# A two-layer attention and mixture-of-experts kernel: down products in other pieces, norm rows spread by TensorE

## The reference

```python
for layer in range(2):
    h = attention[layer](x)
    x = layernorm(ALPHA * x + h, ln_g[layer, 0], ln_b[layer, 0])
    f = moe(x, w_gate[layer], w_up[layer], w_down[layer])
    x = layernorm(ALPHA * x + f, ln_g[layer, 1], ln_b[layer, 1])

def moe(t):                       # combine: two gates a token, chosen by a router
    for e in range(32):           # w_gate, w_up: 1024 x 256, w_down: 256 x 1024
        h = silu(t @ w_gate[e]) * (t @ w_up[e])
        y = y + combine[:, e:e + 1] * (h @ w_down[e])
```

## Time and profile before

| | us |
|---|---|
| median of 3 runs (lowest to highest) | 701.18 (700.98 to 702.95) |
| the profiled execution | 701.19 |
| its span | 699.4 |
| TensorE busy | 644.9 |
| VectorE, ScalarE, GpSimd busy | 298.1, 194.9, 141.0 |

### The profile page before, as it was taken

One profiled execution on the slowest core, in us unless ns is written; L12 is line 12 of the kernel. 1 busy time (PEld: TensorE's weight loads), 2 busy tenths in 40 slices (PEclk: granted clock), 3 DMA queues, 4 the chain that ended last, 5 costly groups with the idle time before them and its releaser, 6 DMA issues.

```text
span 699.4 us, 9577 instructions
## 1 busy us (share of the span) xinstructions
PE 644.9 (92%) x3586; PEld 372.0 (53%) x3588; DVE 298.1 (43%) x644; ACT 194.9 (28%) x398; POOL 141.0 (20%) x159
## 2 busy tenths in 40 slices
PE   8999999999999989889989988999999998888993
PEld 6969878664333333335548966865433333333551
DVE  4768745743332322222256565675332322131125
ACT  4658661531101100100147245353110100010012
POOL 0504110062101001000058790006210100110001
PEclk9999999999999999999999999999999999999998
DMA  9990049899999999999997029289999999999992
GB/s 327 366 381 4 1 170 420 346 376 393 369 420 422 421 420 422 420 421 422 403 419 295 1 88 425 97 359 381 394 368 421 420 421 421 423 419 422 421 399 80
DMA packets 44029, 237.76 MB, mean 340 GB/s; under 512 B 3968, under 2 KB 4144, under 8 KB 20432
## 3 DMA queue, kind: packets, MB, share of 16 engines
q1 hardware_dynamic: 42976, 235.40, 83.0%
q10 hardware_dynamic: 576, 1.05, 0.5%
q0 software_dynamic: 432, 0.70, 0.3%
HBM read 236.08 MB, written 1.05 MB: 339 GB/s over the span
## 4 chain that ended last, share of the span: by engine, by line
PE 57%; DMA 26%; SPq 7%; DVE 5%; ACT 3%; issue 2%; DVEq 0%; ACTq 0%
PE psum L627 54%; DMA ring<-in_moe_w_up 23%; SPq L503 5%; DMA ring<-in_diff_w_qkv 3%; ACT ring_rounded L1457 1%; SPq L508 1%; PE psum L1123 1%; DVE ln_stats L1792 1%; SPq L488 1%; PE psum L1015 1%; SPq L490 1%; PE psum L963 0%; ACT scratch L1359 0%; DVE psum L1818 0%; DVE small L2087 0%
## 5 line engine op out<-in xcount | busy, mean ns | idle before, releaser
L627 PE MATMUL psum<-ring,work 128*64 128x512 f32 (+2 forms) x1360 | 237.2, 501 | 26.3 <-DMA ring<-in_moe_w_up 23.6
L627 PEld LDWEIGHTS psum<-ring,work 128*64 128x64 f32 (+1 forms) x1360 | 105.0, 140 | 158.4 <-issue 134.8
L627 PE MATMUL psum<-ring,scratch 128*64 128x512 f32 x512 | 122.0, 598 | 1.8 <-ACT scratch L1616 1.8
L2314 DVE SCALAR_TENSOR_TENSOR scratch<-psum,small,scratch 128x256 f32<-128x256 f32 x30 | 14.5, 484 | 209.6 <-ACT scratch L1610 209.6
L2425 POOL COPY work<-work 128x512 f32 x60 | 37.2, 624 | 290.3 <-PE psum L627 276.3
L1610 ACT ACTIVATE scratch<-psum 128x256 f32<-128x256 f32 x32 | 12.3, 383 | 263.0 <-PE psum L627 263.0
L627 PEld LDWEIGHTS psum<-ring,scratch 128*64 128x64 f32 x512 | 35.3, 136 | 64.6 <-issue 55.3
L627 PE MATMUL psum<-ring_rounded 128*128 128x256 f32 (+2 forms) x230 | 66.3, 308 | 0.0
L627 PE MATMUL psum<-ring_rounded,x_T_rounded 128*128 128x512 f32 x192 | 60.9, 398 | 0.0
L627 PE MATMUL psum<-x_T_rounded,ring_rounded 128*128 128x256 f32 x256 | 44.8, 285 | 0.3 <-ACT ring_rounded L1324 0.3
L627 PEld LDWEIGHTS psum<-ring_rounded 128*128 128x128 f32 x230 | 41.8, 191 | 2.0
(11 more groups left out here) (290 smaller groups left out, 820.1 us busy)
## 6 DMA issues: line engine op xcount, KB each, us to landing
ring<-in_moe_w_gate SPq DMA_DIRECT2D x60, 1024.0 KB, 20.9
ring<-in_moe_w_up SPq DMA_DIRECT2D x60, 1024.0 KB, 22.6
ring<-in_moe_w_down SPq DMA_DIRECT2D x60, 1024.0 KB, 20.0
ring<-in_diff_w_qkv SPq DMA_DIRECT2D x5, 2048.0 KB, 20.7
ring<-in_diff_w_o SPq DMA_DIRECT2D x1, 4096.0 KB, 19.4
ring<-in_moe_w_down SPq DMA_DIRECT2D x8, 512.0 KB, 16.3
ring<-in_mla_w_o SPq DMA_DIRECT2D x1, 4096.0 KB, 34.8
ring<-in_moe_w_gate SPq DMA_DIRECT2D x4, 768.0 KB, 6.6
```

The costliest lines, as they stand in the source:

```text
L627: return pe.matmul(dst, lhsT, rhs, start=start, stop=stop, skip_group_check=True)
L2314: dve.scalar_tensor_tensor(out=h_sb, in0=up, scalar=gate_col, in1=act_s, op0=ALU.mult, op1=ALU.mult).then_inc(m["h_ready"], 1)
```

## The change

The first three pairs do both halves of their down at once (`FIRST_SPLIT`), so that pairs 1 to 3 combine before their transpose and have no half left over from the pair before. The norm's four half rows are loaded once, into one partition each; TensorE spreads two of them over 128 partitions with a product of a row of ones (`scale_rows`), the first two after `rows(1)` of pair 0 and the others after pair 1's transpose, into banks that the first combine opens later; VectorE multiplies and adds for both token tiles from PSUM; ScalarE's and GpSimd's part of it goes. The last pair's down is loaded, multiplied, evicted and added in lots of 512, 256 and 256 columns, in banks 4, 5 and 6. Semaphores are renamed and counted accordingly (`x_dve`, `x_pool` become `x_first`, `x_second`).

```diff
+FIRST_SPLIT = 3
+GB_BANKS = ((2, 3), (1, 3))
+LAST_DOWN_COLS = (slice(0, 512), slice(512, 768), slice(768, 1024))
+LAST_DOWN_BANKS = (4, 5, 6)
-        gb_half = top.rearrange("p (s n) -> p s n", s=2)
+        gb_rows = [top[32 * r:32 * r + 1, 0:512] for r in range(4)]
...
                 sp.wait_ge(*mo[l]("offs_ready", 1))
-                for i, w in enumerate((ln_g, ln_b)):
-                    sp.dma_start(gb_half[:, i, :], w[l, 0, 0:512].partition_broadcast(P)).then_inc(ld_gb, 16)
+                for r, row in enumerate(gb_rows):
+                    w, cols = (ln_g, ln_b)[r // 2], slice(r % 2 * 512, (r % 2 + 1) * 512)
+                    sp.dma_start(row, w[l, 0, cols].rearrange("(a n) -> a n", a=1)).then_inc(ld_gb, 16)
...
-                for c in range(2):
-                    cols = slice(c * 512, (c + 1) * 512)
+                for c, cols in enumerate(LAST_DOWN_COLS):
                     for j in range(2):
                         sp.dma_start(slot_dn(s, j)[:, :, cols], moe_w_down[l, expert(i, j)]
...
+                def scale_rows(half):
+
+                    pe.wait_ge(*gb_loaded(l, 1))
+                    for r, bank in zip((half, 2 + half), GB_BANKS[half]):
+                        last = mm(psum[:, bank, :], ones[32 * r:32 * r + 1, :], gb_rows[r], True, True)
+                    last.then_inc(m["gb_ps"], 1)
+
                 def combine(n, c):
 
+                    if n == 0:
+                        for t in range(TT):
+                            pe.wait_ge(*scaled((x_first, x_second)[t], l, c))
...
                             rows(1)
+                            scale_rows(0)
...
-                    if i == 1:
-                        combine(0, 0)
+                    if 1 <= i <= FIRST_SPLIT:
+                        combine((i - 1) // 2, 1 - i % 2)
                         transpose()
-                    elif 1 < i < PAIRS - 1:
+                        if i == 1:
+                            scale_rows(1)
+                    elif FIRST_SPLIT < i < PAIRS - 1:
                         down(i - 1, 1)
                         transpose()
                         combine((i - 1) // 2, 1 - i % 2)
...
                         down(i, 0)
-                        if first:
+                        if i < FIRST_SPLIT:
                             down(i, 1)
                     else:
-                        pe.wait_ge(last_down, 32 * (l + 1))
-                        down(i, 0)
-                        pe.wait_ge(*rings[l][s]("dn", turn * 32))
-                        down(i, 1)
+                        pe.wait_ge(*m("y_act", i + 1))
+                        pe.wait_ge(*m("y_dve", i + 1))
+                        for n, cols in enumerate(LAST_DOWN_COLS):
+                            if n < len(last_down):
+                                pe.wait_ge(last_down[n], 32 * (l + 1))
+                            else:
+                                pe.wait_ge(*rings[l][s]("dn", turn * 32))
+                            down_cols(s, i % 2, cols, LAST_DOWN_BANKS[n], True, True).then_inc(m["y_ps" if n else "y0_ps"], 1)
...
-                act.wait_ge(*scaled(x_dve, l, 0))
-                act.wait_ge(*scaled(x_pool, l, 0))
-                for i, w in enumerate((ln_g, ln_b)):
-                    act.dma_start(gb_half[:, i, :], w[l, 0, 512:D].partition_broadcast(P)).then_inc(ld_gb, 16)
...
-                upper(n + 1, 0, PAIRS)
-                upper(n + 1, 1, PAIRS)
+                act.wait_ge(*m("y0_ps", PAIRS))
+                act.wait_ge(*m("c_ps", 2 * (SETS - 1)))
+                act.copy(half(0), psum[:, 4, :]).then_inc(m["y_act"], 1)
+                for k, cols in enumerate(LAST_DOWN_COLS[1:]):
+                    act.wait_ge(*m("y_ps", PAIRS + k))
+                    act.copy(y_hi[:, cols], psum[:, LAST_DOWN_BANKS[1 + k], 0:cols.stop - cols.start]).then_inc(m["y_act"], 1)
...
             def scale_shift_half(l, half):
 
                 cols = slice(half * 512, (half + 1) * 512)
-                dve.wait_ge(*gb_loaded(l, half))
-                chain(dve.tensor_tensor(xs[:, 0, cols], xs[:, 0, cols], gb_half[:, 0, :], ALU.mult))
-                dve.tensor_tensor(xs[:, 0, cols], xs[:, 0, cols], gb_half[:, 1, :], ALU.add)\
-                   .then_inc(x_dve, 1)
+                g, b = GB_BANKS[half]
+                dve.wait_ge(*mo[l]("gb_ps", half + 1))
+                for t in range(TT):
+                    chain(dve.tensor_tensor(xs[:, t, cols], xs[:, t, cols], psum[:, g, :], ALU.mult))
+                    dve.tensor_tensor(xs[:, t, cols], xs[:, t, cols], psum[:, b, :], ALU.add)\
+                       .then_inc((x_first, x_second)[t], 1)
...
-                scale_shift_half(l, 0)
...
                 weights(1)
+                scale_shift_half(l, 0)
                 for i in range(1, PAIRS, 2):
                     odd_pair(i)
-                    if i == 3:
+                    if i == 1:
                         scale_shift_half(l, 1)
...
                 lower(SETS - 1, 0)
-                lower(SETS - 1, 1)
+                for k, cols in enumerate(LAST_DOWN_COLS[1:]):
+                    part = slice(cols.start - 512, cols.stop - 512)
+                    dve.wait_ge(*m("y_act", 2 * SETS + k))
+                    dve.tensor_tensor(y_lo[1][:, part], psum[:, LAST_DOWN_BANKS[1 + k], 0:cols.stop - cols.start],
+                                      y_hi[:, cols], ALU.subtract)\
+                       .then_inc(m["y_dve"], 1)
...
                 windows(1, False, 0, m["xg_ready"])
-                scale_shift_half(l, 0)
                 pair(2, 2)
                 pair(3, 3)
-                scale_shift_half(l, 1)
```

More of the change, by code:

```diff
@@ L406, in build @@
         sems = [{n: sem(f"ring_{n}{s}") for n in ("gate", "up", "dn")} for s in range(SLOTS)]
-        last_down = sem("last_down")
+        last_down = [sem(f"last_down{n}") for n in range(len(LAST_DOWN_COLS) - 1)]
         last_up = [sem(f"last_up{n}") for n in range(len(LAST_UP_PARTS) - 1)]
@@ L561, in moe @@
                                      .rearrange("(p k) n -> p k n", p=P)[:, :, cols])\
-                          .then_inc((last_down, rings[l][s]["dn"])[c], 16)
+                          .then_inc((*last_down, rings[l][s]["dn"])[c], 16)
             def overflow(l, more):
                 with sp.If(more):
-                    sp.wait_ge(*mo[l]("y_ps", PAIRS))
+                    sp.wait_ge(*mo[l]("y_ps", PAIRS + 1))
                     def step(i, r, n):
@@ L604, in _ @@
             sp.wait_ge(mq["b_ps"], 12)
-            sp.wait_ge(*scaled(x_dve, 0))
-            sp.wait_ge(*scaled(x_pool, 0))
+            sp.wait_ge(*scaled(x_first, 0))
+            sp.wait_ge(*scaled(x_second, 0))
             load_pair(1, 0, 0)
@@ L617, in _ @@
                 cols = slice(c * 512, (c + 1) * 512)
-                for t, done in ((0, x_pool), (1, x_dve)):
+                for t, done in ((0, x_second), (1, x_first)):
                     sp.wait_ge(*scaled(done, 1, 2 + c))
@@ L1124, in transpose_h, with down_cols, down_half @@
                     return last
-                def down_half(s, b, c, opens, closes):
+                def down_cols(s, b, cols, bank, opens, closes):
                     for k in range(FF // P):
                         for j in range(2):
-                            last = mm(psum[j * WIN:(j + 1) * WIN, 4 + c, :], hT[b][:, k, j * WIN:(j + 1) * WIN],
-                                      slot_dn(s, j)[:, k, c * 512:(c + 1) * 512], opens and k == 0,
+                            last = mm(psum[j * WIN:(j + 1) * WIN, bank, 0:cols.stop - cols.start],
+                                      hT[b][:, k, j * WIN:(j + 1) * WIN], slot_dn(s, j)[:, k, cols], opens and k == 0,
                                       closes and k == FF // P - 1)
                     return last
+                def down_half(s, b, c, opens, closes):
+                    return down_cols(s, b, slice(c * 512, (c + 1) * 512), 4 + c, opens, closes)
                 def down(i, c):
@@ L1239, in moe @@
                     pe.wait_ge(*m("g_ready", SETS))
-                    pe.wait_ge(*m("y_act", 2 * SETS))
-                    pe.wait_ge(*m("y_dve", 2 * SETS))
+                    pe.wait_ge(*m("y_act", 2 * SETS + 1))
+                    pe.wait_ge(*m("y_dve", 2 * SETS + 1))
                     pe.sem_inc(o["free"], 1)
@@ L1268, in moe @@
                     pe.wait_ge(*m("g_ready", SETS))
-                    for c in range(2):
-                        pe.wait_ge(*m("y_act", 2 * SETS - 1 + c))
-                        pe.wait_ge(*m("y_dve", 2 * SETS - 1 + c))
-                        for t in range(TT):
-                            add_rows(t, c, pick_last, stop=True).then_inc(m["sum_ps"], 1)
+                    for n, cols in enumerate(LAST_DOWN_COLS):
+                        pe.wait_ge(*m("y_act", 2 * SETS - 1 + n))
+                        pe.wait_ge(*m("y_dve", 2 * SETS - 1 + n))
+                        c, at_ = divmod(cols.start, 512)
```

(18 more changed lines are left out.)

14 lines of the change are left out of this document (7 added, 7 removed).

## The result

The changed kernel takes 697.39 us in the median of 13 runs (696.53 to 700.02), the kernel before on the same chip 701.25 (13 runs). The ratio is 0.9944, with a 95% interval of 0.9934 to 0.9955: 3.9 us faster. The forecast was 695.5 us, range 692.8 to 698.9.

The account below looks back on a forecast made before the run. Weights over DMA bound the kernel, except at the two ends of an expert stage. Two stages, each gaining 2.45 us at the front and 0.4 at the tail, take 5.7 from 701.19: 695.5 us, range 692.8 to 698.9.

Parts of the forecast that it names:

- the dry place: DMA queue at 176.2 to 181 us, waiting for pair 4's down: only 218 GB/s moved, 2.33 us lost.
- the walk along TensorE: Front of each expert stage: product times summed to date each load request and its flow; gain 2.45 us a stage.
- rival 2: All DMA time saved counts, 5.8 us a stage, with the tail 12.5 in all: 688.7 us; chance 0.05.
- The tail: Last pair of a stage: smaller lots let the statistics start sooner, taken as 0.4 us, ends 0.2 and 0.5.
- Rivals 3 and 4: 3: dry place only moves, S = 2.4, 699.5 us, chance 0.11. 4: late pair 6's down, slower, 705.6 us, chance 0.09.
- Price S: TensorE's time for one spread of two norm rows, four instructions: taken as 1.4 us, ends 0.98 and 1.96.
- A A B B: Instruction order of a spread's two rows on TensorE; one overlapping pair, so three slots of four remain, 1.47 us.
- rival 1: The spread's two rows overlap fully on TensorE, S = 0.98: 7.4 us faster, 693.8 us; chance 0.20.
- Where the front ends: Pair 6's down starts at the latest of 205.80, 205.99 and 206.47 instead of 208.92: 2.45 us gained a stage.
- L = 1.6 us: Lag from a load's issue on an empty DMA queue to the start of its stream.
- 203.67 + 2S: Earliest flow of pair 6's down after TensorE's release; the latest of three bounds, 206.47 us with S = 1.4.
- a dry place of over 1 us at 204 to 208: Sign that the forecast is wrong: the DMA queue running dry for over 1 us at 204 to 208 us.

Follow-up runs that it names:

- the lots alone: Kernel before with only the last down in lots of 512, 256 and 256 columns, neither spread nor order: 701.11 us, ratio 0.9989.
- four downs undivided: Changed kernel with the first four downs undivided instead of three, so pair 6's down is asked for sooner: 697.99 us, ratio 0.9946.
- all three edits: Changed kernel with pair 5's gate asked for sooner, first four downs undivided, first spread behind pair 0's downs: 696.65 us, ratio 0.9923.
- the order alone: Kernel before with only the first three downs undivided; norm rows still copied to all partitions, last down in two halves: 699.08 us, ratio 0.9944.

## Why the prediction was right, and where its sizes were off

**What was right.** The direction, the place and the mechanism: the dry place was pair 4's down, the order took it away, and the walk along TensorE put every request within 0.4 us (with S = 1.06: pair 5's gate 178.91, measured 179.25; pair 6's down 204.19, measured 204.40). VectorE's norm work is hidden, with 2.5 us to spare (163.58 to 166.12). The norm copies' 1.05 MB bring nothing directly: ahead of pair 3's down the queue now runs low, as forecast, and rival 2's 688.7 us is far off. The tail gave 0.47 against 0.4. Rivals 3 and 4 needed S of 2.4 or more.

**Price S.** The step "their instructions come as A A B B: only the second A and the first B can pair" failed. I took 1.4; the spread costs 1.06, close to the 0.98 of a full overlap, and rival 1 had the price right. The Trainium skill ("TensorEngine Tiling (Array Packing)", Key Properties) lets different tiles work in parallel; the price here agrees with that, 1.06 us against the 1.96 of four full-height instructions, and the trace has the four start two at a time. No run shows which two, or whether a single such product would cost half by itself. A and B need not stand side by side, since eight instructions as A A A A B B B B cost 1.92. (The products that I read in the earlier trace rows are of 128 and of 256 columns, mixed alike in both rows, not all of 128.) This error alone would have put the time at 701.19 - 2 x (3.13 + 0.4) = 694.1 us.

**Where the front ends.** The mis-sized term is the 2.45 us of front gain; it measured 1.35 to 2.13. The step that failed is "Pair 6's down starts at the latest of three" with L = 1.6 us: I let a request cost nothing as long as it came before the queue's end, and 1.6 us behind a dry queue. The runs showed a loss in between: asked for 1.5 us ahead, pair 5's gate lost 1.2 us over the next 6 us. The walk's 3.13 less this 1.2 is 1.9; gate 15 landed 2.0 to 2.3 us sooner by the mean of its parts, and the rest went to its last part, which the walk doesn't know. That pair 6's down decides (203.67 + 2S) was not borne out either: asked for 7 us sooner, it gave fronts of 1.90 and 2.19 us, no clear gain on 1.35 to 2.13. (The 1.25 us in this sum are 1.22 by their own rows, 176.85 - 175.63, which moves it by 0.06.) With pair 5's gate 4.9 us ahead and pair 6's down off the path, the walk's 3.13 came out as 2.99. My sign of error, "a dry place of over 1 us at 204 to 208", looked 25 us too late.

**What the sum left out.** The time outside the span was taken as unchanged; it is 0.34 us longer. So was the second attention, which is 1.46 us longer in this trace.

**Smaller lots.** Counted at nothing, and nothing it is: the transfers from gate 15 on run at 391 instead of 401 GB/s, and no product waits. The Trainium skill ("DMA: Bandwidth & Descriptors", Rules for kernel authors) asks for 1 MiB or more a transfer; in this place, with 256 KB, the trace shows no price that reaches the end.

Summed over the mean of the traced fronts, 2 x 1.65, with two tails of 0.47 and 0.34 back: 3.9 us, which is the measured difference. This leaves out the second attention, and so holds only if the low clock there is as frequent before as after, which is not shown.

**What was luck.** Two errors of opposite sign met in the sum: an S of 1.4 took 0.68 us too much off each front (3.13 - 2.45), and the slow stretch and the last part of gate 15, which the sum had at nothing, took off 1.48 (3.13 - 1.65). With the right S alone the forecast would have been 3.3 us below the measured time instead of 1.9.

## What to carry to other kernels

When a dry queue is repaired, walk on to the next request and ask how much work the queue still holds when it comes: here requests 1.1 to 1.9 us ahead of its end lost 0.4 to 1.2 us, and 3.1 to 4.9 us ahead were enough. An edit that only adds work ahead of a release (the spread) is paid for by the edit that moves the release; alone it was slower. Read what a queue gains from all the parts of a load: the last part, for which the engine waits, scattered by more than 1 us between fronts of one kernel. The kernel with pair 5's gate asked for sooner has the lowest ratio, 0.9920 against the changed kernel's 0.9944; their intervals touch at 0.9934 to 0.9935, so that it beats the change is likely and not settled.

## What the hardware showed that was not expected

**The clock in the second attention.** This stretch took 125.35 to 125.68 us in four of the thirteen traces (the kernel before, the lots alone, four downs undivided, all three edits) and 126.75 to 127.41 in nine, whatever had been changed ahead of it. From 360 to 470 us the mean granted clock is 1.00 in each of the four and 0.98 in each of the nine. Two windows of the changed kernel:

```profile
417.00:423.00 6.00, 4.12 (x18) 3.61 (x19) 4.76 (x17) 3.02 (x11) 0.38 (x1) 0.72 1.01 427
419.90:423.10 3.20, 3.02 (x11) 2.75 (x12) 2.56 (x10) 1.97 (x9) 0.00 (x0) 0.50 0.99 417
```

In the timeline of TensorE four products in it:

```profile
420.77 1.49 PE L631 MATMUL psum<-ring,work 128*128 128x256 f32 x4
```

The first window and the same four products in the kernel with four downs undivided:

```profile
417.00:423.00 6.00, 4.90 (x34) 3.90 (x35) 4.04 (x14) 3.68 (x12) 0.00 (x0) 1.00 1.01 426
```

```profile
419.66 0.82 PE L631 MATMUL psum<-ring,work 128*128 128x256 f32 x4
```

The granted clock falls to the 1.2 GHz level for part of the window (0.50 from 419.9 to 423.1 us), after TensorE had waited 1.46 and 1.10 us for VectorE; in the other kernel it waited 1.34 and 1.10 us at this point and stayed at 2.4 GHz, and so it did in the kernel before with 1.47 and 1.10 us. Four products take 1.49 instead of 0.82 us, and the stretch is about 1.5 us longer. That is as much as most of the edits move: with the 0.34 us outside the span it is why the profiled execution of the change, with 3.7 us gained at fronts and tails, is only 1.8 us shorter, and it is likely why edits worth 1 us a stage in the trace were hard to see in the medians. What decides between the two I did not find.

**Time outside the span.** On the mean of their runs the kernel before and the order alone take 1.76 to 1.79 us beside the span, the lots alone 1.88, every kernel with the spread 2.14 to 2.18. The spread also takes ScalarE's transfers away and adds short ones to SyncE's; which of these it is was not tried.

**A short queue is slow, not idle.** The DMA engines count as 0.95 busy while 337 GB/s come, and a packet takes 0.325 instead of 0.273 us. Why was not settled.
